# A two-block decoder on one core: the second block's mixers go item by item between its linears

## The reference

```python
proj = rms_norm(h, norm_mix) @ w_in              # splits into g_q g_k g_v g_alr g_og c_q c_kv k_pe
log_a = log_sigmoid(g_alr @ gla_gate_w2 + gla_gate_b) / 16
o_gla = rms_norm(gla_chunked(g_q, g_k, g_v, log_a), gla_out_norm) * silu(g_og)   # 4 heads, chunks of 64
q  = rms_norm(rms_norm(c_q) @ mla_w_uq, mla_q_norm)        # 8 heads of 96, the last 32 with rope
kv = rms_norm(c_kv) @ mla_w_ukv                            # 64 + 64 per head
k  = rms_norm(concat(kv_nope, k_pe), mla_k_norm)           # rope on the last 32
o_mla = causal_attention(q, k, v)                          # softmax, query blocks of 128
h = h + concat(o_gla, o_mla) @ w_out
xq = rms_norm(rms_norm(h) @ xa_w_q, xa_q_norm); xk, xv = rms_norm(mem) @ xa_w_kv   # 4 heads of 128
h = h + attention(xq, rms_norm(xk, xa_k_norm), xv) @ xa_w_o
g, u = rms_norm(h) @ ffn_w_gate, rms_norm(h) @ ffn_w_up    # width 2816
h = h + (silu(causal_conv3(g)) * u) @ ffn_w_down
```

## Time and profile before

| | us |
|---|---|
| median of 3 runs | 2462.17 (2461.18 to 2467.87) |
| the profiled execution | 2461.34 |
| its span, first to last instruction | 2459.5 |
| TensorE busy | 2375.6 (97%) |
| VectorE busy | 1720.3 (70%) |
| ScalarE busy | 1264.0 (51%) |
| GpSimd busy | 130.1 (5%) |
| mean granted clock | 0.989 |

### The profile page before, as it was taken

The page is one execution under the profiler, slowest core; times in us unless marked ns, Lnnn a source line. Parts: engine busy times, 40 slices in busy tenths (PEclk is TensorE's granted clock), DMA queues, the critical chain, the costliest instruction groups (busy, mean ns, idle before and its releaser), DMA issues.

```text
span 2459.5 us, 38136 instructions
## 1 busy us (share of the span) xinstructions
PE 2375.6 (97%) x15002; PEld 2130.2 (87%) x15002; DVE 1720.3 (70%) x3142; ACT 1264.0 (51%) x2072; POOL 130.1 (5%) x161
## 2 busy tenths in 40 slices
PE   8999999999999999999999999999999999877999
PEld 7778999999988887776899999998887787556997
DVE  6566599888955555666669988885556667665775
ACT  3454444566644454645444456654545555454444
POOL 0000000022200000000000012220000000000000
PEclk9999999999999999999999999999999999889999
DMA  7455556544466665743555654446666664312665
GB/s 239 145 187 173 162 174 191 177 135 133 129 192 193 205 191 183 233 131 94 172 162 179 188 167 135 131 131 203 191 194 211 184 202 124 111 52 94 189 181 162
DMA packets 111808, 407.86 MB, mean 166 GB/s; under 512 B 12544, under 2 KB 12592, under 8 KB 111376
## 3 DMA queue, kind: packets, MB, share of 16 engines
q1 hardware_dynamic: 108144, 393.13, 52.5%
q0 software_dynamic: 2768, 10.73, 1.3%
q10 hardware_dynamic: 720, 1.57, 0.2%
HBM read 404.33 MB, written 1.05 MB: 165 GB/s over the span
## 4 chain that ended last, share of the span: by engine, by line
PE 85%; DVE 6%; ACT 4%; DMA 4%; issue 1%; ACTq 0%; DVEq 0%
PE ps L532 13%; PE ps L535 13%; PE ps L538 13%; PE ps L600 10%; PE ps L604 10%; PE ps L596 9%; PE ps L813 5%; PE ps L564 3%; PE ps L571 3%; DMA raw<-in_peer_v 3%; PE ps L567 3%; DVE lo L1654 1%; PE ps L641 1%; ACT hi L1148 1%; PE ps L787 1%
## 5 line engine op out<-in xcount | busy, mean ns | idle before, releaser
L1654 DVE TENSOR_TENSOR lo<-raw,hi 128x1024 fp32r<-128x1024 f32 (+1 forms) x689 | 843.3, 1227 | 535.0 <-ACT hi L1148 533.3
L1148 ACT ACTIVATE hi<-raw 128x1024 fp32r<-128x1024 f32 (+1 forms) x689 | 726.9, 1057 | 683.0 <-PE ps L604 295.4
L532 PE MATMUL ps<-xh,hi 128*128 128x256 f32 x2760 | 398.2, 287 | 15.1 <-ACT hi L1148 12.2
L535 PE MATMUL ps<-xl,hi 128*128 128x256 f32 x2760 | 389.0, 284 | 0.0
L538 PE MATMUL ps<-xh,lo 128*128 128x256 f32 x2760 | 387.6, 283 | 0.0
L532 PEld LDWEIGHTS ps<-xh,hi 128*128 128x128 f32 x2760 | 356.2, 192 | 16.2 <-ACT hi L1148 12.2
L535 PEld LDWEIGHTS ps<-xl,hi 128*128 128x128 f32 x2760 | 357.5, 193 | 0.2 <-DVE xl L1773 0.2
L538 PEld LDWEIGHTS ps<-xh,lo 128*128 128x128 f32 x2760 | 356.1, 192 | 0.0
L596 PE MATMUL ps<-hi,lh 128*128 128x512 f32 x1036 | 320.8, 391 | 11.4 <-ACT lh L1185 11.4
L600 PE MATMUL ps<-hi,ll 128*128 128x512 f32 x1036 | 321.4, 391 | 3.0 <-DVE ll L1717 3.0
L604 PE MATMUL ps<-lo,lh 128*128 128x512 f32 x1036 | 319.8, 390 | 0.0
(11 more groups left out here) (305 smaller groups left out, 2313.2 us busy)
## 6 DMA issues: line engine op xcount, KB each, us to landing
raw<-in_peer_u SPq DMA_DIRECT2D x256, 512.0 KB, 3.6
raw<-in_peer_v SPq DMA_DIRECT2D x256, 512.0 KB, 3.7
raw<-in_ret_vg SPq DMA_DIRECT2D x32, 512.0 KB, 4.2
raw<-in_peer_q SPq DMA_DIRECT2D x24, 512.0 KB, 3.6
raw<-in_ffn_gate SPq DMA_DIRECT2D x22, 512.0 KB, 4.0
raw<-in_ffn_up SPq DMA_DIRECT2D x22, 512.0 KB, 4.0
raw<-in_ffn_down SPq DMA_DIRECT2D x22, 512.0 KB, 3.6
raw<-in_ret_qk SPq DMA_DIRECT2D x16, 512.0 KB, 5.3
```

Source lines behind the costliest of these rows:

```text
L532: e.matmul(out, uh[:, k, :], xh[:, k, :], start=k == 0, stop=False)
L535: e.matmul(out, uh[:, k, :], xl[:, k, :], start=False, stop=False)
L1148: e.activation(parts(i)[0][:, 0:w], raw[:, i % N_RAW, 0:w], ACT.Copy).then_inc(s_hi, 1)
L1654: e.tensor_tensor(ul[:, 0:w], raw[:, i % N_RAW, 0:w], uh[:, 0:w].bitcast(F32), ALU.subtract).then_inc(s_lo, 1)
```

## The change

It rewrites the second block on all engines; the first block's code changes in names alone.

- **Units.** `w_in_alr` goes; its 16 columns stand behind w_in_c's, which is 432 wide; they are turned to `alr` (`alrT`). The plain units leave the list: GpSimd's queue loads them into `uq` and `ukv` once the expert layer's left operands are made. The first 512 gate columns of the feed-forward become four token-major units `ffn_first`. Twelve units get places of their own.
- **Linears between.** `w_in_c`, `xa_w_q` and `ffn_first` go by tile (`halves`): all four units for tile 0, then tile 1.
- **Gated linear attention** runs between the units of w_in_v and w_in_og; MLA's query turns stand before the last unit of w_in_og. Generators give way to steps written out between `hi_to` and `lo_to` calls.
- **GpSimd** multiplies the memory keys by root and gains, and the Silu gate by its gains (`og2`). Squares move to ScalarE. MLA's query gains take in the key gains; the k_pe part is roped once, not per head.
- **Attention** (`Pairs`): items with query tile outermost, three buffers of weights instead of two, turned weights of all items kept, values of a whole query tile in one bank, one division for it. Two items run before w_out, two scores ahead; the others between the halves of w_out's first four slices.
- **Output layers** by tile: the 128x512 result of a tile is turned into one bank, and ScalarE and VectorE make hi and lo of it there (`left`), instead of copying it and splitting slice by slice. `w_out` and `xa_w_o` end with four halves of tile 1.
- **Norms by tile** (`rms`): split, residual of tile 0, variance, split, scale, split, residual of tile 1, xl of tile 0, and so on.

The core of the diff (the first is TensorE's, the second VectorE's, the third GpSimd's):

```diff
-            to_xs(X_MIX, xnk, lambda t, g: (s_xn, t + 1))
-            u = claim("alr", UPPER, filled=(s_used, used("w_in_alr", 0)))
-            tok("w_in_c", 0, "cc", X_MIX, width=416, step=lambda s: next(steps, None))
+            halves("w_in_c", "cc", X_MIX, 432)
+            gla_feat(0, 0)
+            turn("alrT", LOWER, [Sec.cc[:, t, 416:432] for t in range(2)], rows=16)
...
-            n = W.first["mla_ukv"]
-            e.wait_ge(*landed(n))
+            e.wait_ge(s_mla, 48)
...
-            tok("w_in_v", 0, "gv", X_MIX)
-            tok("w_in_og", 0, "og", X_MIX)
+            def beside_og(s):
+                if s < 3:
+                    next(linear)
+                if s == 3:
+                    e.wait_ge(s_gla["made_q"], 1)
+                    heads_T("mqT", Sec.mq, 8, 96, LOWER)
+            tok("w_in_v", 0, "gv", X_MIX, step=lambda s: next(linear) if s == 2 else None)
+            tok("w_in_og", 0, "og", X_MIX, step=beside_og)
...
+            next(heads)
+            next(heads)
             e.wait_ge(s_gla["o"], 1)
-            to_T(("woT", 0), lambda t, k: Sec.o[:, t, k * 128:(k + 1) * 128], 4)
-            acc("w_out", 8, attend2, turn_rest)
+            for t in range(2):
+                left_turn("gla", t, Sec.o[:, :, 0:512])
+            for k in range(4):
+                out_half(k, 0)
+                next(heads)
+                if k == 3:
+                    mla_values(0)
+                out_half(k, 1).then_inc(s_used, 1)
+                next(heads)
...
+            halves("xa_w_q", "cq", X_XA, ready=xn_ready(2), beside=lambda s: query_turn(0) if s == 2 else None)
...
+            xs_tile(X_FFN, xnk, xn_ready(6), 0)
+            halves("ffn_first", "fg", X_FFN, ready=xn_ready(6))
```

```diff
+            inverse(rstd[:, 0:8])
+            tt(o4, o4, bc(r3, 3, 128), ALU.mult)
+            e.wait_ge(s_gla["og2"], 1)
+            me.wait()
+            e.tensor_tensor(Sec.o[:, :, 0:512], Sec.o[:, :, 0:512], Sec.og, ALU.mult).then_inc(s_gla["o"], 1)
+            even_T("mkT", Sec.mkT, 2)
...
+            n0 = W.first["xa_w_o"]
+            query_variance(0)
+            lo_to(n0)
+            query_scale(0)
+            heads = pair_heads(pairs["xa"])
+            next(heads)
+            query_variance(1)
+            next(heads)
+            query_scale(1)
+            next(heads)
+            lo_to(n0 + 1)
+            next(heads)
```

```diff
+            e.wait_ge(s_gla["memr"], 1)
+            e.tensor_tensor(v, v, bc(sm[:, 48:56].rearrange("p (t h) -> p t h", t=2), 3, 128), ALU.mult).then_inc(s_pool, 1)
+            e.wait_ge(s_pool, 1)
+            e.tensor_tensor(v, v, over(R_XK), ALU.mult).then_inc(s_gla["mem"], 1)
+            for t in range(2):
+                e.wait_ge(*use["og", t].freed)
+            e.tensor_tensor(og, og, over(R_GLA), ALU.mult).then_inc(s_gla["og2"], 1)
```

More of the change, by code:

```diff
@@ L504, in build @@
             place(W.first["diff_w_out"] + 6 + i, Diff.late[i], (s_scored, 16))
+        place(W.first["w_in_c"] + 3, Tail.more[0], *read("peer_v1", 128))
+        for i in range(3):
+            place(W.first["w_out"] + 5 + i, Sec.spare[i], (s_gla["o"], 1))
+        place(W.first["xa_w_q"] + 3, Tail.more[0], (s_wl, left_count["mla", 1]))
+        for i in range(3):
+            place(W.first["xa_w_o"] + i, Tail.more[1 + i], (s_wl, left_count["mla", 1]))
+        place(W.first["xa_w_o"] + 3, Sec.spare[0])
+        place(W.first["ffn_first"] + 3, Sec.spare[1])
         W.settle()
@@ L1532, in act @@
[L1532 to L1540 removed]
+            n0 = W.first["w_in_c"]
+            to_xs(X_MIX, gain=C_MIX, tiles=(0,))
@@ L1544, in act @@
+            hi_to(n0 + 2)
             for t in range(2):
@@ L1568, in act @@
+            n0 = W.first["w_in_og"]
+            hi_to(n0)
             for t in range(2):
                 evac(("gv", t), Sec.gv[:, t, :])
-            tok_units("w_in_og", 0, lambda s: next(work, None))
+            hi_to(n0 + 1)
+            e.activation(Sec.ckv2, Sec.ckv[:, :, 0:512], ACT.Square).then_inc(s_gla["memsq"], 1)
+            hi_to(n0 + 2)
+            hi_to(n0 + 3)
+            for t in range(2):
+                evac(("gintra", t), Sec.o[:, t, 0:512])
+            root(sm[:, 48:56])
@@ new lines, in act @@
+            query_turn(0)
+            evac(("cq", 1), Xa.cq[:, 1, :])
+            heads = pair_heads(pairs["xa"])
+            next(heads)
+            query_turn(1)
+            next(heads)
+            root(rstd[:, 4:8])
+            next(heads)
+            hi_to(n0 + 1)
+            next(heads)
+            next(heads)
+            left("xa", 0, Xa.left[0])
+            next(heads)
+            hi_to(n0 + 3)
+            left("xa", 1, Xa.left[0])
+            n0 = W.first["ffn_first"]
+            hi_to(n0)
@@ L2293, in dve @@
-            steps = decays()
-            units("w_in_c", 0, 4, lambda s: next(steps, None))
-            for c in range(2):
-                units("w_in_qk", 2 * c, 2, lambda s: next(steps, None))
-            even_T("mkT", Sec.mkT, 2)
+            n0 = W.first["w_in_c"]
+            to_xs(X_MIX, gain=C_MIX, tiles=(0,))
+            lo_to(n0 + 2)
+            to_xs(X_MIX, gain=C_MIX, tiles=(1,))
+            lo_to(n0 + 3)
+            n0 = W.first["w_in_qk"]
+            lo_to(n0)
+            for t in range(2):
+                e.wait_ge(*use["cc", t].freed)
@@ L2352, in dve @@
-            work = prepare()
-            units("w_in_v", 0, 4, lambda s: next(work, None))
-            units("w_in_og", 0, 4, lambda s: next(work, None))
+            n0 = W.first["w_in_v"]
+            lo_to(n0)
+            e.wait_ge(s_gla["ln"], 1)
+            me.wait()
+            me.did(e.scalar_tensor_tensor(out=flat(Sec.z), in0=flat(Sec.za), scalar=-1.0 / 16.0, in1=flat(Sec.z),
+                                          op0=ALU.mult, op1=ALU.add))
+            for f in range(2):
+                me.wait()
+                me.did(e.tensor_tensor_scan(Sec.cum[:, f, :], Sec.scanm, Sec.z[:, f, :], 0.0, ALU.mult, ALU.add))
@@ L2438, in dve @@
-            acc("w_out", 8, lambda k: Sec.oT[:, k, :], before=attend2,
-                after=lambda k: even_T(("woT", 1), Sec.oT[:, 4:8, :], 2) if k == 2 else None, lead=1)
+            linear = gated_linear()
+            n0 = W.first["w_in_og"]
+            lo_to(n0)
+            next(linear)
+            inverse(Sec.qscale)
+            ts(Sec.qscale, Sec.qscale, 96.0 ** -0.5, None, ALU.mult)
+            pe = Sec.cc[:, :, 384:416]
+            tt(pe, pe, bc(Sec.rows[:, R_MK + 64:R_MK + 96], 1, 2), ALU.mult)
@@ L2475, in taps @@
+            left("xa", 1, Xa.left)
+            rms("xa_w_o", W.first["ffn_first"], X_FFN, C_FFN)
+            lo_to(W.first["ffn_first"] + 4)
             def taps(c):
```

1067 lines of the change are left out of this document (534 added, 533 removed).

## The result

| | before | changed |
|---|---|---|
| median, us (lowest to highest) | 2462.3 (2461.2 to 2467.9) | 2437.2 (2436.8 to 2438.1) |
| ratio, 95% interval | | 0.9894 (0.9877 to 0.9911) |
| span of the profiled execution | 2459.5 | 2435.0 |

The account below looks back on a forecast made before the run. The prediction saw 59 us of TensorE idling and low clock in the second block's 212.1 us stretch; five parts ended at 2255.0 against 2278.6, 23.6 off 2459.5, plus 1.8 outside: 2437.7, put as 2437 (2419 to 2452).

Parts of the forecast that it names:

- Part 1: Second block's linears, gate and gated linear attention: 65.3 us of TensorE work plus waits and hand-overs, 71.2, ending at 2124.2.
- under 1 us ahead: At gated linear attention's state updates VectorE leads TensorE by under 1 us; 3 us late there loses 3.
- Part 2: MLA and w_out: 37.2 us of TensorE work plus 16.5 of waits and clock, 53.7, ending at 2177.9.
- the 11 us put down as standing: Ahead of w_out: TensorE stands 6 us for the gate product, then 5 more to the first output matmul.
- GpSimd's product, taken at 3.1: Gate product og2 ahead of w_out: 3.1 us, by 2.5 times VectorE's 1.22; bounds 1.22 and 6.9.
- Parts 3 and 5: Norm with xa_w_q by tile, 19.9 us (before 22.9), and feed-forward start, 20.4 (before 20.8).
- Part 4: Cross attention and xa_w_o: work 21.1, waits 12.7, clock 3, so 36.8 us, 4 worse than before.
- The hole of 8.8: Cross attention: item 1's turned copy leaves ScalarE 8.8 us after TensorE turned it, behind table loads and a split.
- Rival A: Cover nearly full: waits before w_out and in cross attention halve, clock cost mostly goes; 2415 us, chance 0.10.
- Rival B: GpSimd slow, og2 and memory keys 6.9 each: 2444, or 2451; beyond 2450, or Rival C in part, 0.12.
- Rival C: From w_in_v to w_out, 16 units' splits all bare at 2.3 us each: 36.8, 2474 us, chance 0.05.
- D: Nothing gained: Rival C's slips in six or seven units and Rival B together, 2459 us, chance 0.05.

Follow-up runs that it names:

- before_plain: Kernel before with only the three plain MLA units moved out of the raw-buffer ring to GpSimd's queue; 2455.4 us against 2464.5, ratio 0.9963.
- dve_late: Changed kernel with three idle 128x1024 products on VectorE behind the copy of the attention matrix; 2439.0 us, ratio 0.9895.
- pool_more: Changed kernel with two more unread 128x1024 products on GpSimd ahead of og2; 2441.5 us, ratio 0.9907.
- whole_tiles: Changed kernel with xa_w_q and ffn_first not by tile: both tiles turned first, then each unit for both; 2443.6 us, ratio 0.9915.
- xa_both: Changed kernel with xa_w_o's unit 1 split and the second query tile's root moved ahead of cross attention's first exponentials; 2435.0 us, ratio 0.9884.
- xa_turn: xa_both with ScalarE's copy of tile 1's turned queries also ahead of the exponentials of items 0 and 1; 2432.1 us, ratio 0.9868.
- best_order: out_first with ScalarE copying an item's turned weights in cross attention ahead of the exponentials of the item two later; 2422.9 us, ratio 0.9835.
- out_first: xa_turn with GpSimd's og2 replaced by a VectorE product, and memory-key copies, w_out's second hi and first left operand made earlier; 2425.2 us, ratio 0.9840.
- keep_busy: Changed kernel with unread matmuls (six, five and sixteen) at two places ahead of w_out and one in cross attention; 2437.8 us, ratio 0.9887.

## Why the prediction was right

The forecast was 2437, its range 2419 to 2452; measured 2437.2. That the two agree to 0.2 is luck. The working gave 2437.7, rounded down, and the five parts make 202.0 where 199.8 were measured; the stretch began 1.0 later and what follows it took 0.3 more, neither of which was forecast. No part is off by more than 2.0. The parts, each with its own start:

| | predicted | measured | what differs |
|---|---|---|---|
| 1 linears, gate | 71.2 | 70.0 | busy 65.9 for 65.3, waits 4.2 for 4.4, no hand-overs for 1.5 |
| 2 MLA, w_out | 53.7 | 55.7 | values +2.7, small steps +1.8, waits 10.2 for 13.5, clock 3.8 for 3 |
| 3 norm, xa_w_q | 19.9 | 19.2 | clock 1.5 for 2 |
| 4 cross attention, xa_w_o | 36.8 | 35.1 | hole 8.2, waits 10.5 for 12.7, clock 2.0 for 3, work 1.5 more |
| 5 feed-forward | 20.4 | 19.7 | clock 1.5 for 2; the 1.0 of extra turns taken over |

- **Part 1.** The waits are where I put them: xl 2.2, the MLA ups behind a copy 1.0, gv 0.9. No DMA wait is left, and before_plain puts 5.8 us on that. That VectorE is "under 1 us ahead" at the states holds to 0.1 by dve_late; that 3 us of lateness there would be 3 lost was too dear, as 2.5 cost 1.8.
- **Part 2.** From its start to the first output matmul I had 14.3 us by my end points (2124.2 to 2138.5); it was 14.0 (2124.06 to 2138.03). But of the 11 us put down as standing (6 and 5) TensorE stood 7.7 (1.91, 3.31 and 2.50); the other 6.3 was work, part of it at the low clock. The length was right, its make-up was not. GpSimd's product, taken at 3.1, took 2.34 for the gate and 1.90 and 2.40 for the memory keys, near the 2.2 that the prediction worked out from the Trainium skill (GPSIMD Engine Reference, section Performance versus the Vector engine) and left out of the sum. The page's 4497 ns are for a two-input add, where the prediction says a product; page and trace agree, and the ratio of VectorE's and GpSimd's tensor_scalar was a poor guide. (One of the prediction's signs of being wrong, a product outside 2 to 4 us, did come: 1.90. It changes nothing else.) That pool_more follows one for one shows the place right, the size 0.8 too large. The term that was mis-sized the other way is MLA's values, 2.6 predicted for 24 matmuls of 64 columns. The trace shows each of these fp32 matmuls as two records, 48 in all; 32 of them:

```profile
2164.26 3.68 PE L1079 MATMUL ps<-big 128*128 128x64 f32 x32
2167.76 0.71 PE L620 MATMUL ps<-hi,mla_left 128*128 128x512 f32 x2
```

  3.50 us to the next work, 0.11 a record, about as far apart as the ones of 128 columns in cross attention (2.05 for 16 above, the last one's length in it); so 5.3 for all 48. I had halved for the columns. The trace of the kernel before already showed the price, four records in 0.39, 0.10 each, which makes 4.7 for 48:

```profile
2176.62 0.56 PE L708 MATMUL ps<-big 128*128 128x64 f32 x4
2177.01 0.61 PE L641 MATMUL ps<-ident,big 128*128 128x128 f32 x4
```

- **Parts 3 and 5.** Going by tile was worth 6.5 us by whole_tiles, with the clock's share in it; against the kernel before I had found 3.0 and 0.4, the latter after 1.0 of turns. The sums hold to 0.7 each. That the old order had less standing ahead of its turns than whole_tiles has would explain the difference; it was not tested.
- **Part 4.** The hole of 8.8 was 8.2, with the chain as named: xa_both, xa_turn and best_order each took one link out of it, and C fell from 54.3 to 44.9: 5.4 with these edits, and 4.1 with the clock in out_first, where C had no edit. The Trainium skill (ScalarE: Activation LUTs, section What ACT_TABLE_LOAD costs) puts a switch of tables at 2.66 us with a drain behind the load; the trace has the next exponential 0.07 us behind a load of 1.28 (2206.03 and 2207.38 above), so the two loads cost 2.6 here, not the 5.3 of an estimate by the page.
- **Rival A** (holes halved, 2415) did not come, though best_order shows that most of the holes could be had by order alone: 2422.9. (Its "30 us" of waits are 13.5 + 12.7 = 26.2 in the prediction's own terms, without the clock; with them the 22 still comes out.) **Rival B** fell with GpSimd at 2.3. **Rival C** (splits bare) is not seen: TensorE waits for no lo in w_in_og. **D** likewise.

Of the 24.5 us, the runs assign 5.8 to the plain units, 3.3 to the place of gated linear attention and 6.5 to the tiles, some of it clock. The other 9 (one unit fewer, the output layers' left operands, the items between w_out's halves) were not taken apart; the three numbers are also not a clean sum, as one is from the kernel before and two from the changed one.

## What to carry to other kernels

When a chain of small steps decides, list what stands on each engine ahead of the step that TensorE waits for, in queue order; splits, table switches and copies for later work go in front of or behind the chain, and each removal must be followed to the wait that is next. A product that nothing covers belongs on the engine that is idle anyway: VectorE was waiting 3.4 us for GpSimd's gate product and could do its half while ScalarE made the Silu. Compare variants by stages at the same granted clock, not by medians alone, when a few us matter.

## What was unexpected in the hardware

The granted clock behind a short stall was not fixed by the program: of the four profiles with the same program up to w_out two had 1.00 behind the input's turns and two 0.88. Over all 11 profiles, with TensorE 4.1 us from the start of these turns to the first matmul and 2.2 of them waiting, it was 1.00 in 3 and 0.88 in 8, and the stage was 1.5 us longer at 0.88; behind the other two norms 5 and 4 of 11 were full. The Trainium skill (TensorE: Matmul & The Clock Gate, section What's actually happening) says that the chip's watch on the engine runs free of the kernel, so that the point of change differs between runs of one kernel; these profiles agree that it differs, and show no cause. Three such places make 4.6 us between a lucky and an unlucky execution. They are not the whole spread of the runs (keep_busy: 2435.9 to 2441.8): the profile of keep_busy's slowest has 380.3 us in its four stages, 0.7 less than the changed kernel's profile, and is 5.0 longer only because its first block, which no edit touches, ended 5.7 later (2059.7 against 2054.0). And matmuls that nobody reads can be worth their place: 58 of them made the changed kernel 6 us faster by the medians and 3.4 by the two stages that they stand in, though a better order, which shortens the stalls themselves, was worth 14 by the medians.
